# Memory keys normalised one unit earlier, attention heads with fewer turns, and the final gain loaded with x

## The reference, cut to what matters

```python
# first block
mod = silu(c) @ w_ada + b_ada                 # 6 x 2048 values: shifts, scales, gates
h = modulate(rmsnorm(x, g_norm_mix), shift_m, scale_m)
proj = h @ w_in                               # q, k, v of differential attention, latents of MLA
mix = concat(o_diff, o_mla) @ w_out           # 8 + 8 attention heads
x = x + gate_m * mix
h = modulate(rmsnorm(x, g_norm_ffn), shift_f, scale_f)
x = x + gate_f * (square(relu(h @ w_ff1)) @ w_ff2)
x = rmsnorm(x, g_final)
# second block: three branches on the same x
proj = rms_norm(x, norm_gain) @ w_in_2
ya = sliding_window_attention(qa, ka, va)     # 12 heads of 64
yb = forgetting_attention(qb, kb, vb, fb)     # 12 heads of 64
mk, mv = split(rms_norm(mem, mem_norm_gain) @ w_mem_kv)
yc = memory_attention(qc, mk, mv)             # 4 heads of 128, mk is normalised per head
x = x + (g0 * ua + g1 * ub + g2 * uc) @ w_out_2
```

## Time and profile before

| what | value |
|---|---|
| time, median of 3 runs | 2175.58 us |
| lowest and highest run | 2174.42, 2175.61 us |
| the profiled execution | 2174.42 us, its span 2172.6 us |
| PE busy | 1992.0 us (92%) |
| DVE busy | 1314.6 us (61%) |
| ACT busy | 944.5 us (43%) |
| POOL busy | 156.6 us (7%) |
| granted TensorE clock, mean | 0.967 |

### The profile page before, as it was taken

One profiled execution on the slowest core, in us unless ns is written; L12 is line 12 of the kernel. 1 busy time (PEld: TensorE's weight loads), 2 busy tenths in 40 slices (PEclk: granted clock), 3 DMA queues, 4 the chain that ended last, 5 costly groups with the idle time before them and its releaser, 6 DMA issues. The chain is left out here.

```text
span 2172.6 us, 24527 instructions
## 1 busy us (share of the span) xinstructions
PE 1992.0 (92%) x9240; PEld 1635.6 (75%) x9240; DVE 1314.6 (61%) x2057; ACT 944.5 (43%) x1440; POOL 156.6 (7%) x118
## 2 busy tenths in 40 slices
PE   6697896868799999999999999989989999999999
PEld 3376775646577888888888878879888787787877
DVE  3877776776796555555555555567555555545544
ACT  2553444333444344434434445445434444444433
POOL 0000000001100110110010022110100001101000
PEclk9898999879899999999999999999999999999999
DMA  9998675757897555555555565534534456656644
GB/s 354 340 319 294 230 262 194 242 189 262 299 340 261 190 193 185 192 194 184 187 194 190 185 197 172 160 113 139 160 106 150 135 170 190 192 182 187 194 172 168
DMA packets 128967, 448.82 MB, mean 207 GB/s; under 512 B 14288, under 2 KB 14544, under 8 KB 128336
## 3 DMA queue, kind: packets, MB, share of 16 engines
q1 hardware_dynamic: 124928, 433.74, 60.1%
q0 software_dynamic: 1568, 7.34, 0.9%
q10 hardware_dynamic: 2352, 6.17, 0.7%
HBM read 443.00 MB, written 4.19 MB: 206 GB/s over the span
## 5 line engine op out<-in xcount | busy, mean ns | idle before, releaser
L283 DVE TENSOR_TENSOR wlo<-raw,whi 128x1024 fp32r<-128x1024 f32 (+4 forms) x652 | 787.1, 1211 | 736.8 <-ACT whi L282 691.0
L282 ACT ACTIVATE whi<-raw 128x1024 fp32r<-128x1024 f32 (+4 forms) x652 | 657.8, 1011 | 849.4 <-PE g L397 710.5
L392 PE MATMUL g<-whi,lhsA_hi 128*128 128x512 f32 (+4 forms) x1840 | 714.3, 390 | 41.5 <-DVE lhsA_lo L789 34.1
L393 PE MATMUL g<-whi,lhsA_lo 128*128 128x512 f32 (+4 forms) x1840 | 695.5, 380 | 0.0
L397 PE MATMUL g<-wlo,lhsA_hi 128*128 128x512 f32 (+4 forms) x1840 | 467.2, 376 | 0.0
L392 PEld LDWEIGHTS g<-whi,lhsA_hi 128*128 128x128 f32 x1840 | 355.4, 193 | 105.2 <-ACT tmp L781 27.6
L393 PEld LDWEIGHTS g<-whi,lhsA_lo 128*128 128x128 f32 x1840 | 355.5, 193 | 53.7 <-issue 1.4
L397 PEld LDWEIGHTS g<-wlo,lhsA_hi 128*128 128x128 f32 x1840 | 341.6, 191 | 55.9 <-DVE wlo L283 0.2
L537 DVE SCALAR_TENSOR_TENSOR raw<-raw,srow 128x1024 f32<-128x1024 f32 x181 | 216.6, 1219 | 20.5 <-DMA raw<-in_w_ada 20.1
L392 PE MATMUL g<-whi,lhsF_hi 128*128 128x512 f32 x512 | 200.6, 392 | 0.0
L393 PE MATMUL g<-whi,lhsF_lo 128*128 128x512 f32 x512 | 199.3, 389 | 0.0
(11 more groups left out here) (250 smaller groups left out, 1473.2 us busy)
## 6 DMA issues: line engine op xcount, KB each, us to landing
raw<-in_w_ff SPq DMA_DIRECT2D x256, 512.0 KB, 3.5
raw<-in_w_ada SPq DMA_DIRECT2D x181, 512.0 KB, 5.0
raw<-in_w_in SPq DMA_DIRECT2D x176, 512.0 KB, 4.2
raw<-in_w_out SPq DMA_DIRECT2D x64, 512.0 KB, 5.0
raw<-in_w_in SPq DMA_DIRECT2D x80, 384.0 KB, 3.1
raw<-in_w_branch_a SPq DMA_DIRECT2D x12, 512.0 KB, 3.7
raw<-in_w_branch_b SPq DMA_DIRECT2D x12, 512.0 KB, 4.3
raw_wide<-in_w_ada SPq DMA_DIRECT2D x11, 512.0 KB, 8.3
```

Of the source, the lines that this page charges most:

```text
L282: t_hi = AC.put(lambda e: e.activation(hi, x, ACT.Copy), landed, free, us=0.2 + n * 0.00167)
L283: t_lo = DV.put(lambda e: e.tensor_tensor(lo, x, hi.bitcast(F32), ALU.subtract), landed, t_hi, free, us=0.15 + n * 0.00208)
L392: PE.put(lambda e, o=o, x=xh, w=h, f=first: e.matmul(o, x, w, start=f, stop=False), w, mark=False, us=us)
L393: PE.put(lambda e, o=o, x=xl, w=h: e.matmul(o, x, w, start=False, stop=False), mark=False, us=us)
```

## The change

Three things change. The generator `mem_keys` is put in the list right behind the evacuation of `u_mem[0]`, before `row_norms(xs)`, where it stood before `u_h0`; its four empty turns go. One `yield` goes in `softmax_pv` (only where `fold` is given, which is the memory heads), and two in `causal_head`: the transposes of the probabilities follow the exponential in the same turn, and the product with the values follows the copy. And `g_final` is loaded in `reload()`, right behind `x`.

```diff
--- before.py
+++ after.py
@@ -738,8 +738,6 @@
 
     def mem_keys(r, tok):
         yield from heads_norm(r, 4, 128, tok)
-        for _ in range(4):
-            yield
         for j in range(2):
             b = yield from grab(SB)
             k = turn_rows(b, [r.ap[:, t, (2 * j + i) * P:(2 * j + i + 1) * P] for i in range(2) for t in range(2)], r.norm)
@@ -755,6 +753,7 @@
     drain()
     r = take(rows)
     ks = evac2(par, tok, 512, r.ap, t_of["rm"], r.free, scale=(rm[:, 0:1], rm[:, 1:2]))
+    bg.append(mem_keys(r, ks))
     bg.append(row_norms(xs, t_x, ssx, rx, "rx"))
     angles()
     lam()
@@ -1103,7 +1101,6 @@
         bg.append(mla_head(2 * i))
         bg.append(mla_head(2 * i + 1))
 
-    bg.append(mem_keys(r, ks))
     for i in range(6):
         par, tok = run(u_h0[i], width=3)
         t_of["part", i] = evac2(par, tok, 512, part[i], fence)
@@ -1150,6 +1147,7 @@
         w = [PE.tok(), AC.tok(), DV.tok(), PO.tok()]
         t_xr = load(PO, xr[:, :, :], a["x"][0].rearrange("(t p) d -> p t d", p=P), w)
         x_tok.extend([t_xr] for _ in range(4))
+        t_of["gfin"] = load(PO, gfin, a["g_final"].rearrange("(a d) -> a d", a=1).to_broadcast([P, D]), w)
 
     bg.append(reload())
     for u in u_out[0:2]:
@@ -1211,7 +1209,6 @@
     for jc in range(4):
         bg.append(chunk(jc))
     bg.append(spread(1, [DV.tok()]))
-    t_of["gfin"] = load(PO, gfin, a["g_final"].rearrange("(a d) -> a d", a=1).to_broadcast([P, D]), fence)
 
     ssg = sm(8)
     xcnt = [sem("s_xf"), 0]
```

## The result

| | before | after |
|---|---|---|
| median, beside each other on one chip | 2175.0 us | 2191.8 us |
| lowest to highest (4 runs each) | 2172.38 to 2175.61 | 2189.76 to 2192.95 |
| span of the profiled execution | 2172.6 us | 2188.6 us |
| mean granted clock | 0.967 | 0.961 |

The ratio is 1.0078, 95% interval [1.0062, 1.0093]: +16.8 us, where +2.3 was forecast, and outside the range of 2171 to 2187.

A forecast was written before the change was run, and what follows sets the result against it. Transfers were taken to bound the moved generator's stretch (DMA share 0.95), PE the second half. Terms 10.6 - 0.7 - 2.3 - 5.3 + 0 = +2.3 against 2174.42, 2177.9 beside the median: forecast 2178 us, range 2171 to 2187.

The forecast's parts named there:

- Part A: Memory stage, mem_keys moved early: PE stands some 12.4 us for POOL, delaying SP's loads and PE's restart: +10.6 us.
- The assumed slowing of L537 by POOL's squares: Memory stage: POOL squares while DVE is at work, adding 0.8 us to the end of the fourth L537.
- up to 3.98: Memory stage: by the port lock DVE could lose up to all of L733's 3.98 us, changing nothing in the sum.
- Parts B and C: B: u_h0 without its eight transposes, -0.7 us. C: second wait for w_ada, 13.01 us before, gets shorter, -2.3 us.
- Part D: Heads: removed turns save waits for lb and merge two table-load waits: -5.3 us, bounds -7.5 and +5.
- price of turns at once: Heads: PE's transposes following the exponential at once cost 0 to 0.5 us per head, taken as 0.9 for all 24.
- Its first term: Heads: PE's 4.64 us wait for lb goes, with 1.9 us of clock, together -6.5 us.
- The merging of the two waits of 2.7 and 2.0 us: Heads: two waits at loads of an exponential's table become one of about 4.2 us: -0.5 us.
- Part E: g_final loaded behind x: POOL's wait for x stays near 10.2 us, effect 0; +5 if both land together.
- the prediction's own signs of being wrong: Wrong if PE's first wait under 5 us, delay at 99.43 under 4, or pT's waits for an exponential over 5 us.
- The rival that named turns at once after the exponential: Heads: turns at once cost 0.5 us on each of 24, 12 instead of 0.9: near 2189 us, chance 0.07.

The follow-up runs named there:

- m1: Kernel before with only the move of mem_keys: median 2182.7 us, ratio 1.0042.
- h2: Kernel before with both turns of causal_head removed for the a heads only: median 2180.0 us, ratio 1.0027.
- b1: Kernel before with both turns of causal_head removed for the b heads only: median 2172.4 us, ratio 0.9989.
- h1: Kernel before with only the three yields of the heads removed: median 2178.5 us, ratio 1.0022.
- g1: Kernel before with only g_final's load placed behind x: median 2176.6 us, ratio 1.0009.
- m2: Kernel before with mem_keys started early but its four empty turns kept: median 2176.7 us, ratio 1.0010.
- c2_b_second_again: Second run of the kernel before with only the turn ahead of the product with the values removed, b heads only: ratio 0.9969.
- h5: Kernel before with both turns removed for the a heads except heads 3 to 5: median 2180.5 us, ratio 1.0028.
- f1: Kernel before with the gates' exponential and logarithm put into ACT's queue one turn later than DVE's part: ratio 1.0003.

## Why the prediction was wrong, step by step

- **Part A** was right in mechanism and size: 12.4 us of waiting forecast and 13.19 measured, SP's load at 85.3 and 85.86, w_in's first at 97.1 and 97.63, PE's restart at 110.0 and 109.71. The assumed slowing of L537 by POOL's squares did not come (L724 ran from 58.61 to 61.27, before them); instead they began 1.4 us later than in before. That the two numbers agree within 0.8 us owes something to this exchange. Beside L733 two L537 took 2.05 us each for 1.22: DVE lost 1.7 us in all, not up to 3.98, and as expected it changed nothing, since SP stood until 85.86.
- **Parts B and C**: the wait at the second place was 10.87 us, forecast 10.7. With PE's restart 10.3 us late, this wait 2.1 shorter and its end at 208.90 for 202.03, part B is left with -1.3, forecast -0.7. A to C gave +7.6 forecast, +6.8 in the splits. The interval of m1's median allows +6.3 to +12.
- **Part D** failed, and its price of turns at once is the step that made the prediction wrong. It was to give -5.3; alone it costs +4.8, [+2.8, +6.7]: 10.1 of the 14.5 us between forecast and result. Its first term was right as far as the wait goes: lb 6.1 to 1.4. Wrong was the price of turns at once, which I took as 0.9 us for all 24 heads and as a wait for the exponential alone. With the other terms as forecast it would have to be about 11 us (4.8 + 6.5 + 0.5 - 0.8), an estimate; the runs put it in the a heads, +5.9 in h2, while the b heads gave -2.4 in b1 where the lb terms alone were to give -6.5. I bounded it by one head's row, the first head, ahead of the gates and of a row norm. The cost is in the second turn as much as the first: the product waits for the copy on ACT and for the bank that the last head's scaling on DVE frees. Over the 375 us of the a and b heads PE's waits go from 19.3 to 21.6 us in h1's trace. A part is the clock: in the 120 us of the a heads it is 0.94 for 0.97, some 7 us more at the lower level (0.03 x 120 / 0.5), and at 0.28 for 0.41 us per matmul that costs an estimated 2.3 us. Together 4.6; the splits between the 411th and the 531st say 4.4, but 1.6 of these are the clock's step at the 447th, which h1 has and before has not, so the agreement is partly luck.
- The merging of the two waits of 2.7 and 2.0 us, forecast to 4.2, came as 2.6 and 1.4, but with a third of 2.7 right behind.
- **Part E**: x's landing is unchanged (9.91 us of waiting for 10.22), as forecast. The +2.0 of g1 isn't seen there, and its interval takes in nothing.
- None of the prediction's own signs of being wrong came: the first wait was 13.19 us, the delay at the restart 10.3, and waits of pT for an exponential 2.1 in all. The waits that came were of pO, for which there was no sign.
- In the whole change the heads' stretch costs 8.0 us (8.1 to 16.1) where alone it costs 4.4. Of the difference, 3.0 us lie between the 460th and the 475th split, with the same waits of PE in both b stretches: 60.31 us at a granted clock of 0.94 in the changed kernel, 57.29 at 1.00 in h1. It is a step of the clock like that of the last section. m1 and h1 and g1 still add up within their intervals, so no more is claimed.
- The rival that named turns at once after the exponential (2189, chance 0.07) was nearest: it has part A in full and +5.8 us in part D, where +4.8 was measured. But its cause, 0.5 us on each of 24 heads for the exponential, is not what the runs show: the b heads gained, and the waits for an exponential are 2.1 us. It was right in size by luck.

Left open: a second bank for the product would test the wait for z directly. It wasn't tried; the program has its eight accumulation tensors (four `g`, two `pS`, `pT`, `pO`) in use. Nor was it tested why one turn alone costs more at the a heads than both.

## What to carry to other kernels

A yield between two dependent instructions is a place for another engine's work: before removing one, list for each engine what stands between the two, and who frees the buffer the next one needs; the same two turns cost 5.9 us at the a heads, where a row norm and the gates stood near, and gave 2.4 at the b heads, where they took the next head's factor out from behind a norm; there the second of them alone gave 7. Background work moved forward into a stage that waits for transfers must not put an instruction that waits ahead of the one that frees a load's slot. Split such an edit by its loops before timing it as a whole. And where a planner places transfers by the program's order, look at what it did with them before reading an experiment as a change of one thing: in m2 a last batch of three loads in place of seven or eight came with the second wait at 3.69 us for 13.01.

## What the hardware showed that was not expected

The granted clock can fall or not fall in the same stretch with the same instructions and the same waits. Between 1540 and 1600 us, the waits for POOL are 4.8 us and PE is busy 54.4 us in all of before, m1_mem_only, g1_gain_only and m2_mem_early_turns_kept. The stretch in before:

```profile
1540.00:1600.00 60.00, 54.40 (x309) 51.06 (x308) 35.06 (x73) 27.23 (x48) 9.95 (x8) 1.00 0.48 145
```

and in m2_mem_early_turns_kept, 1.2 us early there:

```profile
1540.00:1600.00 60.00, 54.40 (x289) 51.09 (x288) 34.51 (x72) 24.96 (x45) 9.96 (x8) 0.94 0.46 134
```

The clock is 1.00 in one and 0.94 in the other, 309 matmuls are through for 289, and m2's splits go from 1.2 us early to 2.1 late. m1 (6.9 us late) keeps 1.00, g1 (0.1 early) has 0.94. The loss comes in two steps of 1.6 us, one behind each of the two waits for POOL. The first can be compared most closely in c2_b_second_again, whose rows of PE lie within 0.1 us of before's from 1536 us up to there; both have waited 2.3 us until 1550.7. The first row is of before, the second of c2:

```profile
1552.27 0.33 PE L392 MATMUL g<-whi,lhsA_hi 128*128 128x384 f32 x1
1552.30 0.52 PE L392 MATMUL g<-whi,lhsA_hi 128*128 128x384 f32 x1
```

Of the 20 traces of this case four (before, m1, h5, f1) take 30.3 us from the 447th to the 460th split, the others 31.7 to 31.9. The trace of before is of the rarer kind, so a comparison of splits with it across this place charges the other kernel with 1.6 to 3 us that its edit may have nothing to do with; the medians of many runs don't rest on one trace. Chance from run to run, or a shift too small to see here, moves such a kernel by 3 us without any work changed: 27 runs of the kernel before on one chip spread from 2170.71 to 2181.56. That is as large as what g1 and m2 were to show.
